# The low half of each weight panel: a negated copy on ScalarE and accumulating DMAs in place of four GpSimd subtractions

## Time and profile before

| what | value |
|---|---|
| median of the runs | 2135.28 us |
| span of the profiled execution | 2133.8 us, 31557 instructions |
| TensorE busy (matmul) | 2114.8 us, 99% |
| TensorE weight loads | 1794.3 us, 84% |
| VectorE busy | 1469.4 us, 69% |
| GpSimd busy | 1003.7 us, 47% |
| ScalarE busy | 914.6 us, 43% |
| granted TensorE clock | 0.997 of full speed |
| DMA | 202.18 MB, 95 GB/s on average |

### The profile page before, as it was taken

The page is one execution under the profiler, slowest core; times in us unless marked ns, Lnnn a source line. Parts: engine busy times, 40 slices in busy tenths (PEclk is TensorE's granted clock), DMA queues, the critical chain, the costliest instruction groups (busy, mean ns, idle before and its releaser), DMA issues.

```text
span 2133.8 us, 31557 instructions
## 1 busy us (share of the span) xinstructions
PE 2114.8 (99%) x11014; PEld 1794.3 (84%) x11014; DVE 1469.4 (69%) x2016; ACT 914.6 (43%) x1319; POOL 1003.7 (47%) x707
## 2 busy tenths in 40 slices
PE   9999999999999999999999999999999999999998
PEld 7888888777888888887788889988888888899887
DVE  7746556786777777778275787777655556877775
ACT  4423333554655555455445423333354445422333
POOL 4444544455433333435435655555433424655553
PEclk9999999999999999999999999999999999999998
DMA  6232222233222222232312223324222121223231
GB/s 225 87 108 78 87 81 98 90 109 109 85 88 84 79 79 79 79 129 79 119 65 106 90 97 104 112 98 138 79 80 80 60 80 60 99 99 106 100 105 62
DMA packets 38583, 202.18 MB, mean 95 GB/s; under 512 B 4427, under 2 KB 9675, under 8 KB 16236
## 3 DMA queue, kind: packets, MB, share of 16 engines
q1 hardware_dynamic: 34016, 193.56, 26.7%
q10 hardware_dynamic: 4492, 7.60, 1.1%
HBM read 195.90 MB, written 5.24 MB: 94 GB/s over the span
## 4 chain that ended last, share of the span: by engine, by line
PE 88%; DVE 5%; issue 2%; ACT 1%; DVEq 1%; DMA 1%; POOL 1%; SPq 0%; POOLq 0%; ACTq 0%
PE bank L488 14%; PE bank L489 13%; PE bank L494 13%; PE bank L475 10%; PE bank L476 10%; PE bank L477 10%; PE bank L1001 3%; PE bank L995 3%; PE bank L996 3%; PE bank L982 2%; PE bank L987 1%; DVE X L2210 1%; PE bank L1092 1%; DVE T L2207 1%; PE bank L785 1%
## 5 line engine op out<-in xcount | busy, mean ns | idle before, releaser
L406 POOL TENSOR_TENSOR WL<-RAW,WH 128x512 fp32r<-128x512 f32 x700 | 997.4, 1456 | 1102.5 <-ACT WH L1257 1102.5
L1257 ACT ACTIVATE WH<-RAW 128x2048 fp32r<-128x2048 f32 (+1 forms) x190 | 336.5, 1773 | 238.2 <-PE bank L494 121.8
L488 PE MATMUL bank<-HB,WH 128*128 128x512 f32 x776 | 308.1, 397 | 0.8 <-DVEq L2679 0.8
L489 PE MATMUL bank<-HB,WH 128*128 128x512 f32 x776 | 302.6, 390 | 0.0
L494 PE MATMUL bank<-HB,WL 128*128 128x512 f32 x776 | 194.0, 392 | 0.0
L488 PEld LDWEIGHTS bank<-HB,WH 128*128 128x128 f32 x776 | 145.8, 188 | 32.9 <-issue 1.4
L494 PEld LDWEIGHTS bank<-HB,WL 128*128 128x128 f32 x776 | 145.6, 188 | 32.4 <-issue 2.4
L489 PEld LDWEIGHTS bank<-HB,WH 128*128 128x128 f32 x776 | 145.8, 188 | 30.2 <-issue 1.0
L1257 ACT ACTIVATE HIDH<-T 128x512 fp32r<-128x512 f32 x64 | 40.0, 625 | 172.1 <-DVE T L2607 170.8
L1257 ACT ACTIVATE EH<-SUMS 128x1536 fp32r<-128x1536 f32 x24 | 35.7, 1489 | 175.7 <-DVEq L2567 175.7
L475 PE MATMUL bank<-HIDH,WH 128*128 128x512 f32 x256 | 99.7, 390 | 0.0
(11 more groups left out here) (495 smaller groups left out, 5237.3 us busy)
## 6 DMA issues: line engine op xcount, KB each, us to landing
RAW<-panels SPq DMA_DIRECT2D x174, 1024.0 KB, 4.8
xsave<-X ACTq DMA_DIRECT2D x4, 512.0 KB, 2.8
X<-xsave ACTq DMA_DIRECT2D x1, 2048.0 KB, 11.8
TAB<-scratch SPq DMA_DIRECT2D x16, 128.0 KB, 5.4
out<-ACC SPq DMA_DIRECT2D x8, 256.0 KB, 2.3
X<-xin SPq DMA_DIRECT2D x3, 512.0 KB, 9.0
T<-xtok SPq DMA_DIRECT2D x2, 512.0 KB, 11.8
U<-xtok SPq DMA_DIRECT2D x2, 512.0 KB, 13.6
```

The lines of the kernel that those rows point to most:

```text
L406: gp.tensor_tensor(WL[:, s, cs], RAW[:, s, cs], WH[:, s, cs].bitcast(f32), ALU.subtract).then_inc(lo_ready, 1)
L488: nc.tensor.matmul(o, wh[:, columns[k - k0]], xh[:, k, :], start=first and k == k0, stop=False)
L489: nc.tensor.matmul(o, wh[:, columns[k - k0]], xl[:, k, :], start=False, stop=False)
L1257: return nc.scalar.activation(dst, src, ACT.Copy)
```

## The change

GpSimd no longer subtracts. ScalarE, right behind the rounding of a panel, writes the negated and rounded panel into `WL` in two halves of 128 x 1,024, `WL = round(-RAW)`, which is minus the high half. GpSimd then issues, for each half, a DMA from `RAW` to `WL` that adds what it moves to what is there (`accum_op=ALU.add`), so that `WL` ends as `RAW - WH`. Each slot and half has a semaphore of its own that the DMA raises by 16 when it has landed. TensorE waits for these in place of `lo_ready`, by halves now and not by quarters (`PARTS` is 2), and SyncE waits for both halves before it loads the next panel into the slot. GpSimd's loops are written out. To make room for the new semaphores, four small ones of the gating mixer (`rowsum_made`, `wt_split`, `nv_var`, `wt_hi`) are folded into others, with their counts shifted; no work there moves.

```diff
-PARTS = 4
+PARTS = 2
...
+        hi_ready, minus_ready, panel_used = S["panel_hi_ready"], S["minus_high_ready"], S["panel_used"]
+        lo_ready = [[S[f"low_{slot}_{part}"] for part in range(PARTS)] for slot in range(2)]
+        def half_of(part):
+            return slice(part * PANEL // PARTS, (part + 1) * PANEL // PARTS)
...
-                    sp.wait_ge(lo_ready, i * (2 * PARTS) + PARTS * (1 + s))
+                    for done in lo_ready[s]:
+                        sp.wait_ge(done, i * 16 + 16)
...
-            def low_part(s, part):
-                cs = slice(part * PANEL // PARTS, (part + 1) * PANEL // PARTS)
-                gp.tensor_tensor(WL[:, s, cs], RAW[:, s, cs], WH[:, s, cs].bitcast(f32), ALU.subtract).then_inc(lo_ready, 1)
...
+            def low(m):
+                s = m % 2
                 for part in range(PARTS):
+                    cs = half_of(part)
+                    gp.wait_ge(minus_ready, PARTS * m + part + 1)
+                    gp.dma_start(WL[:, s, cs].bitcast(f32), RAW[:, s, cs], accum_op=ALU.add).then_inc(lo_ready[s][part], 16)
+            for m in range(N_MLA + 4):
+                low(m)
...
             def low_up_to(w, c):
-                n, waited = w[2], w[3]
+                value, waited, landed = w[2:5]
                 part = c * PARTS // PANEL + 1
-                if part > waited[0]:
-                    waited[0] = part
-                    pe.wait_ge(lo_ready, n * PARTS + part)
+                while part > waited[0]:
+                    pe.wait_ge(landed[waited[0]], value)
+                    waited[0] += 1
...
+            def minus_high(slot, part):
+                cs = half_of(part)
+                nc.scalar.activation(WL[:, slot, cs], RAW[:, slot, cs], ACT.Copy, scale=-1.0).then_inc(minus_ready, 1)
             def split_panel(m, slot, half):
...
                 hi(WH[:, slot, :], RAW[:, slot, :]).then_inc(hi_ready, 1)
+                for part in range(PARTS):
+                    minus_high(slot, part)
             def split_quarter(m, part, sig=None):
...
+                if part % 2 == 1:
+                    minus_high(slot, part // 2)
```

More of the change, by code:

```diff
@@ L356, in _ @@
             for m in range(2, 6):
-                sp.wait_ge(lo_ready, PARTS * (m - 1))
+                for done in lo_ready[m % 2]:
+                    sp.wait_ge(done, 16 * (m // 2))
                 load(m, m % 2)
@@ L389, in _ @@
                 load_both(i)
-            sp.wait_ge(lo_ready, PARTS * (NPANEL - 2))
+            for done in lo_ready[(NPANEL - 1) % 2]:
+                sp.wait_ge(done, 16 * ((NPANEL - 1) // 2))
             load(NPANEL - 1, (NPANEL - 1) % 2)
@@ L403, in _ @@
         def _(gp):
-            def low_part(s, part):
-                cs = slice(part * PANEL // PARTS, (part + 1) * PANEL // PARTS)
-                gp.tensor_tensor(WL[:, s, cs], RAW[:, s, cs], WH[:, s, cs].bitcast(f32), ALU.subtract).then_inc(lo_ready, 1)
-            def low(s):
+            def low(m):
+                s = m % 2
                 for part in range(PARTS):
[L410 to L429, removed]
+                    cs = half_of(part)
[3 more added lines that the diff above has]
+                low(m)
             gp.wait_ge(S["latent_split"], KQ + KC)
@@ L435, in _ @@
             gp.drain()
[L436 to L440, removed]
+            for m in range(N_MLA + 4, NPANEL):
+                low(m)
             gp.wait_ge(S["norm_hi"], KD * len(SPLIT) + KD + 2)
@@ L458, in panel @@
             def panel(n, slot):
-                return WH[:, slot, :], WL[:, slot, :], n, [0]
+                return WH[:, slot, :], WL[:, slot, :], n * 8 + (16 - 8 * slot), [0], lo_ready[slot], n
             def low_up_to(w, c):
-                n, waited = w[2], w[3]
+                value, waited, landed = w[2:5]
                 part = c * PARTS // PANEL + 1
-                if part > waited[0]:
-                    waited[0] = part
-                    pe.wait_ge(lo_ready, n * PARTS + part)
+                while part > waited[0]:
+                    pe.wait_ge(landed[waited[0]], value)
+                    waited[0] += 1
             def signal(end, sig, last):
@@ L900, in row_sums @@
                     nc.tensor.matmul(bank(4 + j)[:, :], ONES[:, :], WT[:, 4 * j:4 * j + 4, :].rearrange("p g t -> p (g t)"),
-                                     start=True, stop=True).then_inc(S["rowsum_made"], 1)
+                                     start=True, stop=True).then_inc(S["mixed"], 1)
             def mixed(g):
                 if g == 0:
-                    pe.wait_ge(S["wt_split"], 1)
-                    pe.wait_ge(S["mix_split"], NT)
+                    pe.wait_ge(S["mix_split"], NT + 1)
                 o = bank(4 + g % 4)
@@ L932, in _ @@
                     if j == 0:
-                        pe.wait_ge(S["mix_split"], NT + g + 1)
+                        pe.wait_ge(S["mix_split"], NT + g + 2)
                     for f in range(2):
@@ L1745, in _ @@
                 nc.scalar.activation(SQ[:, :, :].rearrange("p a n -> p (a n)"), NV[:, tt, :], ACT.Square,
-                                     accum_out=ST[:, 4, tt:tt + 1]).then_inc(S["nv_var"], 1)
+                                     accum_out=ST[:, 4, tt:tt + 1]).then_inc(S["mix_gelu"], 1)
             split_at(N_MIX + 6)
-            act.wait_ge(S["nv_var"], NT)
+            act.wait_ge(S["mix_gelu"], 8 + NT)
             nc.scalar.activation(ST[:, 5, :], ST[:, 4, :], ACT.Sqrt, bias=EPSC[:, 0:1], scale=1.0 / 1024)\
-                .then_inc(S["nv_var"], 1)
+                .then_inc(S["mix_gelu"], 1)
             for tt in range(NT):
@@ L2450, in _ @@
             half_gate(0)
-            ve.wait_ge(S["nv_var"], NT + 1)
+            ve.wait_ge(S["mix_gelu"], 8 + NT + 1)
             v.reciprocal(inv, root)
@@ L2459, in _ @@
             half_gate(1)
-            ve.wait_ge(S["wt_hi"], 1)
-            lo(WTL[:, :, :], WT[:, :, :], WTH[:, :, :]).then_inc(S["wt_split"], 1)
+            ve.wait_ge(S["mix_hi"], NT + 1)
+            lo(WTL[:, :, :], WT[:, :, :], WTH[:, :, :]).then_inc(S["mix_split"], 1)
             half_gate(2)
             for j in range(2):
-                ve.wait_ge(S["rowsum_made"], j + 1)
+                ve.wait_ge(S["mixed"], j + 1)
                 for g in range(4 * j, 4 * j + 4):
@@ L2473, in low_mixed @@
             def low_mixed(g):
-                ve.wait_ge(S["mix_hi"], NT + g + 1)
+                ve.wait_ge(S["mix_hi"], NT + g + 2)
                 gs = slice(128 * g, 128 * g + 128)
@@ L2481, in _ @@
                     ve.drain()
-                    ve.wait_ge(S["mixed"], g + 1)
+                    ve.wait_ge(S["mixed"], g + 3)
                     ve.wait_ge(S["mix_u_gelu"], g + 1)
```

7 lines of the change are left out of this document (3 added, 4 removed).

## The result

The changed kernel takes 2218.74 us (median of 2 runs, 2218.70 and 2218.78) against 2135.28: ratio 1.0389, 95% interval 1.0359 to 1.0419. It is 83 us slower. The likeliest case of the prediction was +37, 2172 us; the time lies inside its range, but the likeliest case named the wrong side of the 2% bound and less than half the loss.

A forecast was written before the change was run, and what follows sets the result against it. TensorE was taken to bound the kernel, busy 2114.8 of 2133.8 us. Waits for late low halves summed to 39 us, less 2.4 of GpSimd's waits: +37, 2171, or 2172 for the median; range 2138 to 2262.

The forecast's parts named there:

- TensorE's row stays as it is: Whole kernel: no product is taken away, so TensorE's busy time stays at 2115 us.
- ScalarE's copies cost nothing: Each panel's negated copies add 1.92 us on ScalarE, 336 in all, taking it from 43% to about 59%; costed at nothing.
- rival 4: Small tiles, attention stages above all, stand behind ScalarE's 1.92 us of copies: +10 to +30, 2150 to 2200; chance 0.05.
- Landing 5.8 and 8.9 us after the rounding: Every panel: its first half is there 5.8 us after its rounding ends (0.96 + 4.8), its second 8.9.
- Panel by panel: Gaps from rounding to first product with WL, over 175 panels: 10 first halves under 5.8, 20 second under 8.9; sum 39 us.
- "Nothing for TensorE": Load of panel m+2 waits for both low halves and is 3 us late; costs TensorE nothing.
- Nothing in the loops: Halved chunks, 48 panels: gaps of 7.25 to 9.7 us all exceed the landings of 5.8 and 8.9, so no cost.
- rival 2: Halved loops: additions share the 16 engines with loads and land late, from 5.7 us on; 2180 to 2260 and over; chance 0.23.
- VectorE's stretch ends, worth at most 3 us: VectorE's 128x512 instruction falls from 1684 to about 700 ns without GpSimd's reading beside it; 3 us at most.
- Adding at half the rate of copying: Skill's rule for adding DMAs, two source reads: by it the sum is +25 to +40, by a plain copy's rate +5.
- Rivals 1 and 3: 1: additions land like plain copies, +3 to +15, chance 0.24; 3: DMA engines saturate, 2260 to 2500, 0.10.
- rival 5: GpSimd's DMA issue waits for VectorE, each half 0.7 to 1.7 us late: +64 to +100, 2195 to 2235; chance 0.03.

The follow-up runs named there:

- e5_long: Kernel before, with eight extra GpSimd subtractions ahead of those of 12 panels in the halved chunks, making long pauses; 2244.9 us, ratio 1.0507.
- e5_short: Kernel before, with five extra GpSimd subtractions ahead of those of 12 panels in the halved chunks, making short pauses; 2168.8 us, ratio 1.0151.
- e3_plain: Changed kernel with DMAs that copy RAW over WL in place of adding, ScalarE's negated copies kept; 2162.3 us, ratio 1.0124.
- e6b_loops: Changed scheme for the 48 panels of the halved chunks only, GpSimd subtracting for the other 127; 2139.1 us, ratio 1.0015 to the kernel before.
- e1_thin: Kernel before, with GpSimd's four subtractions of a panel cut from 512 to 16 columns each from panel 2 on; 2127.2 us, ratio 0.9958.
- e2_copies: Changed kernel with ScalarE's negated copies kept but no adding DMA, GpSimd subtracting four times a panel as before; 2191.5 us, ratio 1.0257.
- the square: Four kernels: the changed one (adding DMAs, ScalarE's copies) 2218.7 us; with copying DMAs 2162.3; without ScalarE's copies, adding 2199.5 and copying 2141.6.

## Why the prediction was wrong, step by step

The sum's one large term, 39 us of waits on the adding DMAs, held (43.3). What failed are two terms that it put at nothing: TensorE's busy time, which rose by 25.4 us, 16.4 of them by the clock; and ScalarE's copies, which cost 19 to 21 us. (The two overlap: the second price has the clock behind its waits in it.) A third, the later loads, cost 3.2 us and a stretch at the lower clock at one panel.

- **TensorE's row stays as it is**: failed. "TensorE busy stays at 2115" became 2140. The sum had no term for the clock behind a wait, and it is 16.4 us of the 82.8. With `e5_long` the rate is 33 us for 77 of waits, and over before the changed kernel shows 25 for 57, the 9 us that are not the clock among them; with the short pauses of `e5_short` the clock is 5 for 27.
- **ScalarE's copies cost nothing**: failed. They cost 19 to 21 us, with the clock in it. What I had checked, the fourth hidden tile of a chunk, did hold (`HIDH` and `HIDL` bring no wait in the changed kernel, though `HIDL` brings one of 1.3 us in `e3_plain`). The places that did not are single ones outside the loops: `AL` 2.4, `DPL` 3.0, `PJ` 1.9 us. An idle share of 57% was used as evidence against rival 4, though for the low halves the prediction itself went panel by panel and not by shares; that rival, at 0.05, took place beside the forecast, at the middle of its +10 to +30.
- **Landing 5.8 and 8.9 us after the rounding**: right in the median, 6.1 and 8.8 over the 175 panels, and at panel 145 (5.95 to TensorE's product); too short in a crowd, where a half took up to 17.1 from its issue. The page's 6.2 mixes first halves (4.7) with second ones that queue behind them (6.5), so it is no sign against the 4.8. The engine time was near too: 2 x 2.76 us of additions a panel where 6.2 were forecast.
- **Panel by panel**: right in sum and mostly in place. 39 us were forecast for the waits on these DMAs and 43.3 came; from TensorE's waits taken by stretch, the start 12.0 (10.3 forecast), retention heads 6.4 (5.8), first per-layer input 5.7 (6.4), first attention pair 6.0 (3.1), second per-layer input and mixer 6.6 (6.1), start of dilated attention with the loop's last panel, 122, 3.5 (3.4), second wide product 3.2 (4.1). Of the five panels shown, 35 and 145 came near the forecast (3.5 us for 4.0 and 3.2 for 2.75), panel 2 at 5.0 for 3.7, and 7 and 44 at 0 and 0.3 for 1.5 and 2.9. The first attention pair is panel 43's crowd. In the retention heads the total agrees by accident: 5.6 us of it stand at panels 4, 10 and 18, and only 0.8, at panel 31, at the four that were named, 7, 15, 23 and 31.
- **"Nothing for TensorE" of the load that goes out later**: failed at panel 42, by 3.2 us. The load went out 13 us behind the rounding of panel 40, not 8.9, and took 8.3 us. In the loops it held: VectorE's sums wait 34 us for the loads there, and TensorE not at all.
- **Nothing in the loops**: right, within 4 us (`e6b_loops`), so rival 2 is out: its clause of sharing the engines is true, but the landings in the loops stay inside the gaps. That the measured time lies in its 2180 to 2260 is luck. A window of one stretch there, changed kernel:

```profile
1253.00:1298.00 45.00, 45.00 (x200) 37.28 (x199) 25.43 (x28) 29.18 (x25) 6.88 (x8) 1.00 0.79 190
```

- **VectorE's stretch ends, worth at most 3 us**: right in the row, a little small in price (`e1_thin`). The instruction of rows 10 in the changed kernel:

```profile
L2555 DVE TENSOR_TENSOR SUMS<-RAW 128x512 f32<-128x512 f32 x24 | 16.4, 684 | 0.0
```

  But it was no side matter: with GpSimd still subtracting, ScalarE's copies go with a loss of 56 and not 20 (`e2_copies` against the square), as far as the later subtractions are not part of that.
- **Adding at half the rate of copying**: the rule of the Trainium skill (Collectives: The Full Stack, The bandwidth ceiling) agrees with the trace, 2.1 times the engine time and 6.2 against 3.4 us to land. Rivals 1 and 3 are out by the same rows: the adding did not hide, and the engines were not full but in single windows.
- **VectorE holds up the issue** (rival 5): the issue takes 859 ns in the median and 1,241 at most, so not so.

The 82.8 us of span in one line: 43.3 waits on the adding DMAs, less 2.4, 16.5 other waits (8.0 on tiles, 4.0 `EVERY`, 3.2 a late load), 16.4 clock, 9.0 of busy time that stays argued. Why `xsave<-X` lands in 6.8 us for 2.8 and the small `EVERY` 4 us late, I put down to the same crowded engines; no run separated it. No version tried beats the kernel before; `e1_thin` does, but leaves work out, and shows what a low half made for next to nothing would bring, 8 us.

## What to carry to other kernels

Where TensorE bounds a kernel, a wait costs more than its length, since products behind it can run at 1.2 GHz: here four tenths again for waits of 6.5 us, and two tenths on average for waits of 2.2. An engine's idle share says nothing on what a longer step on it costs: go through the small tiles that stand behind each call of the step, in every stage and not only in the loops. A latency that fits the gaps in a steady loop is lost at the few places where the loop starts; there the old way can be kept, and here 39 of 175 panels kept that way took back three quarters of the loss. And before a median is held against a forecast, see whether it mixes cases that the forecast kept apart.

## What the runs showed of the hardware

- An accumulating DMA of 512 KB within SBUF, issued by GpSimd, lands 4.5 us after the start of its issue at best; the first of two in a row lands after 4.7 in the median, the second, issued 0.95 us later, after 6.5. For copying ones it is 2.8 at best, 2.9 and 3.4. Its issue holds GpSimd for 864 ns against 529. The Trainium skill (DMA: Bandwidth & Descriptors, Anatomy of one DMA — SWDGE (gpsimd) path) gives a DMA of GpSimd 2.0 us and its bytes at 436 GB/s; by that page the estimate for 512 KB is 3.2 us, and 4.4 with twice the bytes. The least landings here, 2.8 and 4.5 us, agree within 0.4.
- In the median the loads of `RAW` kept their pace beside the additions, 4.9 us for 4.8, but of the 168 in the loops of SyncE 23 took over 6.5 us where 4 did before, and one of those cost TensorE 3.2 us. Late too were the adding DMAs issued behind a load, and the small transfers.
- The granted clock fell behind 12 of 12 idle stretches of 6.2 to 6.6 us, and behind 3 of 12 of 1.7 to 2.6.
